# Float32 matmuls against three float32r matmuls of halves in a retention kernel on TensorE

## The chip, the cores and the metric

The kernel runs on one core of a Trainium2 chip. The metric is the device time of one execution in microseconds (us), taken as the median of several runs; lower is better. A profiled execution on the chip is also at hand, with the start and duration of every instruction on every engine: TensorE (PE, and PEld for its weight loads), VectorE (DVE), ScalarE (ACT), GpSimd (POOL) and SyncE (SP), which here only issues transfers.

## The reference, cut to what matters

The program is two layers of a hybrid model and a third block, on 512 positions of width 1024, all in float32. A layer normalises x, multiplies it by a wide weight matrix, and feeds three branches: a depthwise convolution of 31 taps, a retention branch with 4 heads, and windowed attention. The change touches retention alone:

```
q = rotary(q, positions, RET_THETA, RET_QK_DIM)      # 4 heads of 256
k = rotary(k, positions, RET_THETA, RET_QK_DIM)      # then k / 16
scores = einsum('bhnid,bhnjd->bhnij', qc, kc) * decay_inner
inner  = einsum('bhnij,bhnjv->bhniv', scores, vc)    # v: 512 per head
...                                                  # forward and backward, summed
mu  = mean(o, axis=-1); var = mean(square(o - mu))
o   = (o - mu) * rsqrt(var + EPS) * silu(gate)
```

The kernel computes forward and backward, and the parts between chunks, in one product: a full 512 x 512 matrix of scores per head, each multiplied by a decay that depends on the distance of its two positions alone. The mean over the value dimension is taken off v beforehand.

## The kernel before, in words

**Weights.** All weight matrices come as 478 slabs of 128 x 1024. SP brings a slab into one of two `raw` buffers; ACT rounds it to float32r (`high`, L911, into `whi`, four buffers); POOL subtracts (`low`, L292, into `wlo`); and PE multiplies in three float32r matmuls, high by high, high by low and low by high (`gemm`, L359 to L361). Eight such triples, 24 matmuls of 512 columns, make a slab's product, in one of the four PSUM banks `gem`. A bank is free again when its semaphore `evac` has counted the read of it. A `raw` buffer is free when POOL has made the low half from it.

**A head of retention.** Each engine has its own program, and semaphores tie them together. For head hd: PE makes four slabs of q and k, ACT copies them to `QK` (`qk_tick`); DVE rotates them in place (`rope`, L1726 to L1732), with `TT` for scratch; PE makes the values in four slabs over all four banks, ACT copies them with their sums to `VT` (`values`, L1052); DVE takes off the mean (`center_values`, L1759). Then `gates`: PE alternates the four gate slabs with four score tiles (`scores`, L492, two matmuls each of k by q, in the banks `xp` 2 and 3) and four value products (`pv`, L503, four matmuls each, in `xp` 0 and 1). DVE makes the argument of the decay (`decay_arg`, L1716 and L1718), ACT its exponential `DT` (L1062), and DVE multiplies each score tile by it into `ST` (`mask_scores`, L1738). ACT reads the products into `OT` and squares them; DVE adds the squares, PE sums them over partitions (`var`), ACT makes the root, DVE the gated halves (`gated`), and PE multiplies by the output weights (`ret_out`, four slabs of halves in all four banks), which DVE adds to `yr` (`add_out`). The scores and the value products are the matmuls in float32; they take their operands from `U`, one large scratch tile that `QK`, `OT`, `ST`, `SG`, `TT`, `VT` and `DT` are parts of.

**Order.** Heads 0 to 2 of a layer are turns of a loop (`Fori`) that holds the gates of head hd, the q, k and values of head hd + 1, and the output product of head hd; head 3 follows apart. In the same time DVE does the convolution by taps, one instruction each, in PSUM: the first four of eight channel tiles before the first head (`early_conv`, L1655, in pieces between the GLU products), the last four in the heads (`conv`, L1702, 27 taps behind the masking, the last four behind the sum of squares). Everything on an engine runs in the order in which it is written. A turn on DVE is decay_arg, mask_scores, conv, sum_squares, gate_products, conv, rope of q, gated, rope of k, center_values, add_out.

**Idle tiles.** `zhi` and `zlo`, eight tiles of 512 columns each, hold in this stage only the gated halves (tiles 0 to 3) and the sum of squares (tile 7). In layer 1 they are called `hhi` and `hlo`.

Of the kernel before, what the change touches and what calls it, by code (L numbers as in the profile page):

```python
# [19 lines left out]
P = 128  # L20
# [11 lines left out]
HEAD_CUT = 27  # L32
PLAIN = 4
# [41 lines left out]
def build(nc, ins, out, xsave):  # L75
# [5 lines left out]
    with ctx:  # L81
# [24 lines left out]
        U = sb("U", [P, U_SIZE])  # L106
        gem = ctx.enter_context(nc.psum_tensor("gem", [P, 4, T], f32))
# [24 lines left out]
        VT = tiles(U_VT, 4)  # L132
        DT = U[:, U_DT:U_DT + 896]
# [52 lines left out]
        def sem(name):  # L186
# [29 lines left out]
            "v_done", "v_sums", "v_ready", "score_done", "st_ready"))  # L216
        vt_done, vt_ready = sem("vt_done"), sem("vt_ready")
# [123 lines left out]
        def _(pe):  # L341
# [81 lines left out]
            def layer(L):  # L423
# [61 lines left out]
                def scores(hd, j):  # L485
                    n = L * 16 + hd * 4
                    if j == 0:
                        pe.wait_ge(roped, L * 8 + hd * 2 + 2)
                    if j >= 2:
                        pe.wait_ge(st_ready, n + (j - 1))  # L490
                    for r in range(2):
                        mm = pe.matmul(xp[:, 2 + j % 2, :], QK[:, 2 + r, j * P:(j + 1) * P], QK[:, r, :],  # L492
                                       start=(r == 0), stop=(r == 1))
                    mm.then_inc(score_done, 1)

                def pv(hd, v):
                    if v == 0:
                        pe.wait_ge(v_ready, L * 4 + hd + 1)
                        pe.wait_ge(st_ready, L * 16 + hd * 4 + 4)
                    if v >= 2:  # L500
                        pe.wait_ge(o_ready, L * 16 + hd * 4 + (v - 1))
                    for j in range(4):
                        mm = pe.matmul(xp[:, v % 2, :], VT[:, j, v * P:(v + 1) * P], ST[:, j, :],  # L503
                                       start=(j == 0), stop=(j == 3))
# [16 lines left out]
                def var(hd):  # L521
                    pe.wait_ge(ossq, L * 4 + hd + 1)
                    pe.matmul(xp[:, 1, :], ones_r[:, :], zhi[:, 7, :], start=True, stop=False)
                    pe.matmul(xp[:, 1, :], ones_r[:, :], zlo[:, 7, :], start=False, stop=True)\
# [371 lines left out]
        def _(act):  # L896
# [91 lines left out]
            def layer(L):  # L988
                g0, u0 = L * LAYER_GROUPS, L * LAYER_USES

                act.wait_ge(consts, 7)
# [52 lines left out]
                def values(G, hd):  # L1044
                    for k in range(4):
                        high(G, 4 + k + 3)
                    for tb in range(4):
# [6 lines left out]
                    act.drain().then_inc(v_sums, 1)  # L1054

# [4 lines left out]
                def gates(G, hd):  # L1060
# [3 lines left out]
                    for k in range(4):  # L1064
# [6 lines left out]
                        read(k, SG[:, k, :], A.Silu)  # L1071
                    log_exp()
# [11 lines left out]
                values(G, 0)  # L1084
                with act.Fori(0, 3) as hd:
# [9 lines left out]
                    values(G + 1, hd + 1)  # L1095
                    for k in range(4):
# [402 lines left out]
        def _(dve):  # L1499
# [117 lines left out]
            def layer(L):  # L1617
# [70 lines left out]
                early_conv(EARLY_GLU * EARLY_PIECE, EARLY * TAPS)  # L1688
# [31 lines left out]
                def rope(G, u, r):  # L1720

                    x1, x2 = QK[:, 2 * r, :], QK[:, 2 * r + 1, :]
                    cos, sin = tab[:, 0, :], tab[:, 1, :]
                    dve.wait_ge(evac[2 * r], u + 1 + PRIMED)
                    dve.wait_ge(evac[2 * r + 1], u + 1 + PRIMED)
                    tt(TT[:, 0, :], x1, cos, O.mult)  # L1726
                    tt(TT[:, 1, :], x2, sin, O.mult)
                    tt(TT[:, 2, :], x2, cos, O.mult)
                    tt(TT[:, 3, :], x1, sin, O.mult)
                    dve.drain()  # L1730
                    tt(x1, TT[:, 0, :], TT[:, 1, :], O.subtract)
                    tt(x2, TT[:, 2, :], TT[:, 3, :], O.add).then_inc(roped, 1)  # L1732

                def mask_scores(hd):
                    dve.wait_ge(dt_ready, L * 4 + hd + 1)
                    for j in range(4):
                        dve.wait_ge(score_done, L * 16 + hd * 4 + (j + 1))
                        tt(ST[:, j, :], xp[:, 2 + j % 2, :], DT[:, 384 - j * P:896 - j * P], O.mult)\  # L1738
                            .then_inc(st_ready, 1)

                def sum_squares(hd):
# [7 lines left out]
                    dve.tensor_copy(zhi[:, 7, :], TT[:, 2, :])  # L1749
# [705 lines left out]
```

## Time and profile before

| | |
|---|---|
| median of 3 runs | 3052.14 us (3050.22 to 3052.88) |
| span of the profiled execution, first to last instruction | 3048.6 us |
| PE busy | 3016.2 us (99%), 13900 matmul records |
| DVE busy | 1695.3 us (56%) |
| ACT busy | 1132.5 us (37%) |
| POOL busy | 1412.8 us (46%) |
| mean granted clock of TensorE | 0.998 |

The profiled execution's own time is known only by its span; the median of the runs lies 3.5 us above that. Busy is the time in which an engine has at least one instruction under way. Matmuls overlap (a record of a 512-column float32r matmul lasts 0.39 us while the next starts earlier), so paces are read from starts and not from durations.

### The profile page before, as it was taken

What the parts mean: (1) busy time and instruction counts of PE and PEld (TensorE: products, weight loads), DVE (VectorE), ACT (ScalarE), POOL (GpSimd) and SP (SyncE); (2) the same over time, 40 slices, a digit from 0 to 9 for tenths busy, and PEclk for the clock granted to TensorE, in tenths of its full rate; (3) what the DMA queues carried; (4) which work ended last, traced back from release to release, by engine and by line L of the source; (5) the groups of instructions that cost most, each with busy time, mean ns of one, the idle gap of its engine ahead of it and who ended that gap; (6) DMA issues with size and microseconds to landing.
All of it is one profiled execution on the core that took longest, in us unless ns stands there. A gap on an engine that the chain in (4) does not pass through costs nothing.

```text
span 3048.6 us, 41069 instructions
## 1 busy us (share of the span) xinstructions
PE 3016.2 (99%) x13900; PEld 2394.0 (79%) x13900; DVE 1695.3 (56%) x2607; ACT 1132.5 (37%) x1714; POOL 1412.8 (46%) x1040
## 2 busy tenths in 40 slices
PE   8999999999999999999999999999999999999998
PEld 6877877877888887777777788878888888788886
DVE  7974575675434597576577644267772253621214
ACT  4233332365332423233245534236563333422223
POOL 5443543455555453443444555453434444454544
PEclk9999999999999999999999999999999999999999
DMA  4222222212222332222221132221213323233222
GB/s 149 97 69 69 96 69 79 87 43 84 97 97 96 127 104 69 97 72 66 83 90 56 36 131 96 93 100 63 83 62 103 98 83 104 83 103 97 96 97 90
DMA packets 73270, 267.87 MB, mean 88 GB/s; under 512 B 8128, under 2 KB 9024, under 8 KB 72768
## 3 DMA queue, kind: packets, MB, share of 16 engines
q1 hardware_dynamic: 70560, 254.84, 25.3%
q10 hardware_dynamic: 2592, 11.46, 1.0%
q8 instruction: 74, 1.21, 0.2%
q14 instruction: 44, 0.36, 0.0%
HBM read 262.07 MB, written 4.19 MB: 87 GB/s over the span
## 4 chain that ended last, share of the span: by engine, by line
PE 83%; issue 7%; POOL 5%; DVE 3%; DVEq 1%; ACT 0%; POOLq 0%; ACTq 0%
PE gem L359 18%; PE gem L361 18%; PE gem L360 18%; POOL wlo L292 5%; PE xp L503 4%; PE gem L749 2%; PE gem L751 2%; PE gem L750 2%; PE xp L492 2%; PE gem L480 2%; PE gem L479 2%; PE gem L478 2%; PE gem L592 2%; PE gem L615 1%; PE xp L651 1%
## 5 line engine op out<-in xcount | busy, mean ns | idle before, releaser
L292 POOL TENSOR_TENSOR wlo<-raw,whi 128x512 fp32r<-128x512 f32 x956 | 1317.4, 1400 | 1571.9 <-ACT whi L911 1571.3
L911 ACT ACTIVATE whi<-raw 128x1024 fp32r<-128x1024 f32 x478 | 504.6, 1056 | 678.2 <-PE gem L361 462.2
L359 PE MATMUL gem<-zhi,whi 128*128 128x512 f32 x1680 | 664.8, 396 | 0.3 <-DVE zlo L1513 0.3
L361 PE MATMUL gem<-zhi,wlo 128*128 128x512 f32 x1680 | 654.0, 389 | 0.0
L360 PE MATMUL gem<-zlo,whi 128*128 128x512 f32 x1680 | 653.7, 389 | 0.0
L359 PE MATMUL gem<-hhi,whi 128*128 128x512 f32 x1296 | 514.1, 397 | 0.0
L361 PE MATMUL gem<-hhi,wlo 128*128 128x512 f32 x1296 | 504.5, 389 | 0.0
L360 PE MATMUL gem<-hlo,whi 128*128 128x512 f32 x1296 | 504.3, 389 | 0.0
L359 PEld LDWEIGHTS gem<-zhi,whi 128*128 128x128 f32 x1680 | 315.5, 188 | 70.8 <-issue 6.0
L360 PEld LDWEIGHTS gem<-zlo,whi 128*128 128x128 f32 x1680 | 315.5, 188 | 70.0 <-issue 5.5
L361 PEld LDWEIGHTS gem<-zhi,wlo 128*128 128x128 f32 x1680 | 315.4, 188 | 66.1
L359 PEld LDWEIGHTS gem<-hhi,whi 128*128 128x128 f32 x1296 | 243.3, 188 | 55.4 <-issue 5.8
L360 PEld LDWEIGHTS gem<-hlo,whi 128*128 128x128 f32 x1296 | 243.4, 188 | 54.8 <-issue 5.3
L361 PEld LDWEIGHTS gem<-hhi,wlo 128*128 128x128 f32 x1296 | 243.3, 188 | 51.0
L920 ACT ACTIVATE U<-gem 128x512 f32<-128x512 f32 x150 | 89.2, 597 | 459.5 <-PE gem L361 437.0
L1702 DVE SCALAR_TENSOR_TENSOR xp<-cv,sm,xp 128x512 f32<-128x512 f32 x224 | 159.1, 752 | 17.2 <-issue 15.0
L1655 DVE SCALAR_TENSOR_TENSOR xp<-cv,vec,xp 128x512 f32<-128x512 f32 x224 | 159.1, 753 | 9.9 <-issue 0.9
L920 ACT ACTIVATE U<-gem,vec 128x512 f32<-128x512 f32 x96 | 65.6, 685 | 233.9 <-PE gem L361 210.5
L2266 DVE TENSOR_TENSOR U<-gem,U 128x512 f32<-128x512 f32 x22 | 15.2, 692 | 185.5 <-PE gem L361 185.5
L503 PE MATMUL xp<-U 128*128 128x512 f32 x256 | 112.4, 592 | 0.0
L749 PE MATMUL gem<-zhi,whi 128*128 128x512 f32 x256 | 106.5, 416 | 0.5 <-POOL wlo L292 0.5
L301 POOL TENSOR_SCALAR U<-U,sm 128x384 f32<-128x384 f32 x64 | 82.1, 1294 | 42.4 <-DVE sm L1898 42.4
(331 smaller groups left out, 3958.5 us busy)
## 6 DMA issues: line engine op xcount, KB each, us to landing
raw<-in_slabs SPq DMA_DIRECT2D x478, 512.0 KB, 3.5
U<-in_x SPq DMA_DIRECT2D x4, 512.0 KB, 7.5
U<-in_x ACTq DMA_DIRECT2D x1, 2048.0 KB, 8.4
xsave<-U ACTq DMA_DIRECT2D x1, 2048.0 KB, 6.5
U<-xsave ACTq DMA_DIRECT2D x1, 2048.0 KB, 8.3
out_y<-yr SPq DMA_DIRECT2D x8, 256.0 KB, 2.2
tab<-in_tab_ret ACTq DMA_DIRECT2D x2, 512.0 KB, 7.8
tab<-in_tab_att ACTq DMA_DIRECT2D x2, 512.0 KB, 3.6
```

Of the source, the lines that this page charges most:

```text
L292: part = pool.tensor_tensor(wlo[:, k % 4, c], raw[:, k % 2, c], whi[:, k % 4, c].bitcast(f32), O.subtract)
L301: last = pool.tensor_scalar(PB[c][hf], PB[c][hf], REC[c][:, hf:hf + 1], None, O.mult)
L359: pe.matmul(o, wh, hi, start=(n == 0), stop=False)
L360: pe.matmul(o, wh, lo, start=False, stop=False)
L361: mm = pe.matmul(o, wl, hi, start=False, stop=(n == len(terms) - 1))
L478: pe.matmul(o, hhi[:, k, c], wh, start=(k == 0), stop=False)
L503: mm = pe.matmul(xp[:, v % 2, :], VT[:, j, v * P:(v + 1) * P], ST[:, j, :], start=(j == 0), stop=(j == 3))
L749: pe.matmul(gem[:, k, :], wh, hhi[:, r, :], start=(r == 0), stop=False)
L911: act.activation(whi[:, k % 4, :], raw[:, k % 2, :], A.Copy).then_inc(hi_done, 1)
L920: act.activation(dst, gem[:, b, :], func, bias=bias, scale=scale).then_inc(evac[b], 1)
L1655: stt(acc if n < TAPS - 1 else TT[:, 0, :], v, w, acc, O.mult, O.add)
L1702: stt(acc if n < TAPS - 1 else TT[:, 0, :], v, w, acc, O.mult, O.add)
```

## The change

Scores and value products are made in three float32r matmuls of halves each. For this q and k are split after rope (ACT the high half into `zhi` 4 to 7, DVE the low half into `zlo` 4 to 7), the masked scores too (DVE multiplies in place in PSUM, ACT writes the high half and DVE the low half of two tiles at a time, into tiles 0 to 3), and the centred values (high halves over `QK`, low halves over `ST`, by a second name `Ur` of the scratch tile). The sum of squares moves from tile 7 to tile 0. PE waits for two masked tiles at a time. Rope works on both halves of q or of k at once, in two instructions of 1024 columns and two of 512. The last 7 taps of `early_conv` move behind the first rope. In the loop, ACT makes the high half of q before its copies for the values, and that of k in their middle.

```diff
+LATE = 7
+        Ur = nc.alloc_sbuf_tensor_at("Ur", [P, U_SIZE], f32r, offset=nc.sbuf_base - 4 * U_SIZE)
+        VHI, VLO = (Ur[:, a:a + 4 * T].rearrange("p (a b) -> p a b", a=4) for a in (U_A, U_C))
...
                 def scores(hd, j):
                     if j == 0:
-                        pe.wait_ge(roped, L * 8 + hd * 2 + 2)
+                        pe.wait_ge(qk_ready, L * 8 + hd * 2 + 2)
                     if j >= 2:
-                        pe.wait_ge(st_ready, n + (j - 1))
+                        pe.wait_ge(st_ready, L * 8 + hd * 2 + 1)
+                    o, c = xp[:, 2 + j % 2, :], slice(j * P, (j + 1) * P)
                     for r in range(2):
-                        mm = pe.matmul(xp[:, 2 + j % 2, :], QK[:, 2 + r, j * P:(j + 1) * P], QK[:, r, :],
-                                       start=(r == 0), stop=(r == 1))
+                        pe.matmul(o, zhi[:, 6 + r, c], zhi[:, 4 + r, :], start=(r == 0), stop=False)
+                        pe.matmul(o, zhi[:, 6 + r, c], zlo[:, 4 + r, :], start=False, stop=False)
+                        mm = pe.matmul(o, zlo[:, 6 + r, c], zhi[:, 4 + r, :], start=False, stop=(r == 1))
...
                 def pv(hd, v):
-                        pe.wait_ge(st_ready, L * 16 + hd * 4 + 4)
+                        pe.wait_ge(st_ready, L * 8 + hd * 2 + 2)
...
                     for j in range(4):
-                        mm = pe.matmul(xp[:, v % 2, :], VT[:, j, v * P:(v + 1) * P], ST[:, j, :],
-                                       start=(j == 0), stop=(j == 3))
+                        pe.matmul(o, VHI[:, j, c], zhi[:, j, :], start=(j == 0), stop=False)
+                        pe.matmul(o, VHI[:, j, c], zlo[:, j, :], start=False, stop=False)
+                        mm = pe.matmul(o, VLO[:, j, c], zhi[:, j, :], start=False, stop=(j == 3))
...
+                def qk_highs(hd, r):
+                    act.wait_ge(roped, L * 8 + hd * 2 + (r + 1))
+                    act.activation(zhi[:, 4 + 2 * r:6 + 2 * r, :], QK[:, 2 * r:2 * r + 2, :], A.Copy).then_inc(qk_high, 1)
-                def values(G, hd):
+                def values(G, hd, mid=False):
                     for k in range(4):
                         high(G, 4 + k + 3)
+                        if mid and k == 1:
+                            qk_highs(hd, 1)
...
+                def value_highs(hd):
+                    act.wait_ge(v_mean, L * 4 + hd + 1)
+                    for tb in range(4):
+                        act.activation(VHI[:, tb, :], VT[:, tb, :], A.Identity, bias=VM[:, tb:tb + 1]).then_inc(v_high, 1)
...
                         read(k, SG[:, k, :], A.Silu)
+                        if k < 2:
+                            act.wait_ge(st_mul, L * 8 + hd * 2 + (k + 1))
+                            act.activation(zhi[:, 2 * k:2 * k + 2, :], xp[:, 2:4, :], A.Copy).then_inc(st_high, 1)
...
                 values(G, 0)
+                qk_highs(0, 0)
+                qk_highs(0, 1)
+                value_highs(0)
...
                     qk_tick(G + 1, 3)
-                    values(G + 1, hd + 1)
-                    for k in range(4):
+                    qk_highs(hd + 1, 0)
+                    values(G + 1, hd + 1, True)
+                    high(G + 3, 3)
+                    value_highs(hd + 1)
+                    for k in range(1, 4):
                         high(G + 3, k + 3)
...
-                early_conv(EARLY_GLU * EARLY_PIECE, EARLY * TAPS)
+                early_conv(EARLY_GLU * EARLY_PIECE, EARLY * TAPS - LATE)
+                def late_conv():
+                    early_conv(EARLY * TAPS - LATE, EARLY * TAPS)
...
+                def rope_low(hd, r):
+                    dve.wait_ge(qk_high, L * 8 + hd * 2 + (r + 1))
+                    c = slice(4 + 2 * r, 6 + 2 * r)
+                    tt(zlo[:, c, :], QK[:, 2 * r:2 * r + 2, :], zhi[:, c, :].bitcast(f32), O.subtract).then_inc(qk_ready, 1)
 
                 def mask_scores(hd):
                     dve.wait_ge(dt_ready, L * 4 + hd + 1)
-                    for j in range(4):
-                        dve.wait_ge(score_done, L * 16 + hd * 4 + (j + 1))
-                        tt(ST[:, j, :], xp[:, 2 + j % 2, :], DT[:, 384 - j * P:896 - j * P], O.mult)\
-                            .then_inc(st_ready, 1)
+                    for a in range(2):
+                        for j in range(2 * a, 2 * a + 2):
+                            dve.wait_ge(score_done, L * 16 + hd * 4 + (j + 1))
+                            o = xp[:, 2 + j % 2, :]
+                            last = tt(o, o, DT[:, 384 - j * P:896 - j * P], O.mult)
+                        last.then_inc(st_mul, 1)
+                        dve.drain()
+                        dve.wait_ge(st_high, L * 8 + hd * 2 + (a + 1))
+                        c = slice(2 * a, 2 * a + 2)
+                        tt(zlo[:, c, :], xp[:, 2:4, :], zhi[:, c, :].bitcast(f32), O.subtract).then_inc(st_ready, 1)
...
                 def center_values(hd):
                     dve.wait_ge(v_sums, L * 4 + hd + 1)
-                    ts(VM, VS, -1.0 / T, None, O.mult)
+                    ts(VM, VS, -1.0 / T, None, O.mult).then_inc(v_mean, 1)
                     dve.drain()
                     for tb in range(4):
-                        last = ts(VT[:, tb, :], VT[:, tb, :], VM[:, tb:tb + 1], None, O.add)
+                        dve.wait_ge(v_high, L * 16 + hd * 4 + (tb + 1))
+                        last = stt(VLO[:, tb, :], VT[:, tb, :], VM[:, tb:tb + 1], VHI[:, tb, :].bitcast(f32),
+                                   O.add, O.subtract)
...
                 rope(G, u, 0)
-                dve.drain()
                 rope(G, u, 1)
+                rope_low(0, 0)
+                rope_low(0, 1)
+                late_conv()
                 dve.drain()
                 center_values(0)
...
                     rope(G + 1, u + 1, 0)
                     gated(hd)
+                    rope_low(hd + 1, 0)
                     rope(G + 1, u + 1, 1)
+                    rope_low(hd + 1, 1)
```

How this moves instructions on DVE before the first head of layer 0, from the last taps of the early convolution to centring. Before (L1655 and L1660 are taps and their closing sum, L1726 to L1732 rope, L1756 and L1759 centring):

```order
L1655 SCALAR_TENSOR_TENSOR xp<-cv,vec,xp 128x512 x28
L1655 SCALAR_TENSOR_TENSOR U<-cv,vec,xp 128x512
L1660 SCALAR_TENSOR_TENSOR cv<-xp,vec,U 128x512
L1726 TENSOR_TENSOR U<-U,tab 128x512
L1727 TENSOR_TENSOR U<-U,tab 128x512
L1728 TENSOR_TENSOR U<-U,tab 128x512
L1729 TENSOR_TENSOR U<-U,tab 128x512
L1731 TENSOR_TENSOR U<-U 128x512
L1732 TENSOR_TENSOR U<-U 128x512
```

And with the change, from the same tap on (L1686 and L1691 taps and sum, L1760 to L1764 rope, L1771 the low halves of q and k, L1801 and L1805 centring); the rope of k repeats the four rows of that of q:

```order
L1686 SCALAR_TENSOR_TENSOR xp<-cv,vec,xp 128x512 x22
L1760 TENSOR_TENSOR U<-U,tab 128x1024
L1761 TENSOR_TENSOR U<-U,tab 128x1024
L1763 TENSOR_TENSOR U<-U 128x512
L1764 TENSOR_TENSOR U<-U 128x512
...
L1771 TENSOR_TENSOR zlo<-U,zhi 128x1024 x2
L1686 SCALAR_TENSOR_TENSOR xp<-cv,vec,xp 128x512 x6
L1686 SCALAR_TENSOR_TENSOR U<-cv,vec,xp 128x512
L1691 SCALAR_TENSOR_TENSOR cv<-xp,vec,U 128x512
L1801 TENSOR_SCALAR sm<-sm 128x4
L1805 SCALAR_TENSOR_TENSOR Ur<-U,sm,Ur 128x512 x4
```

Six taps, the last tap and the closing sum now stand between rope and centring; `decay_arg` still follows centring.

On ACT, in the loop, from the copy that follows the root of the variance (L928 reads q and k) to the reads of the values (L1068). With the change:

```order
L928 ACTIVATE U<-gem 128x512
L1056 ACTIVATE zhi<-U 128x1024
L919 ACTIVATE whi<-raw 128x1024
...
L919 ACTIVATE whi<-raw 128x1024
L1056 ACTIVATE zhi<-U 128x1024
...
L919 ACTIVATE whi<-raw 128x1024
...
L919 ACTIVATE whi<-raw 128x1024
...
L1068 ACTIVATE U,sm<-gem 128x512
```

Before, the same stretch had the four weight copies (L911) in a row and the four reads (L1052) behind them:

```order
L920 ACTIVATE U<-gem 128x512
L911 ACTIVATE whi<-raw 128x1024
...
L911 ACTIVATE whi<-raw 128x1024
...
L911 ACTIVATE whi<-raw 128x1024
...
L911 ACTIVATE whi<-raw 128x1024
...
L1052 ACTIVATE U,sm<-gem 128x512
```

The two copies of 1024 columns (L1056) are new; the second stands between the second and the third weight copy and waits for the rope of k.

## Rows read from the trace of the kernel before

**Rows 1.** The page: busy time, and the chain that ended last.

```profile
PE 3016.2 (99%) x13900; PEld 2394.0 (79%) x13900; DVE 1695.3 (56%) x2607; ACT 1132.5 (37%) x1714; POOL 1412.8 (46%) x1040
...
PE 83%; issue 7%; POOL 5%; DVE 3%; DVEq 1%; ACT 0%; POOLq 0%; ACTq 0%
```

**Rows 2.** PE's groups by form: records, busy us, mean ns, idle before.

```profile
L503 PE MATMUL xp<-U 128*128 128x512 f32 x256 | 112.4, 592 | 0.0
...
L492 PE MATMUL xp<-U 128*128 128x512 f32 x128 | 57.6, 593 | 0.7 <-DVE U L1732 0.7
```

**Rows 3.** PE's timeline, first head of layer 0: start us, us, instruction, idle before.

```profile
149.89 0.39 PE L361 MATMUL gem<-hhi,wlo 128*128 128x512 f32 x1
...
153.29 0.39 PE L361 MATMUL gem<-hhi,wlo 128*128 128x512 f32 x1
154.38 3.70 PE L492 MATMUL xp<-U 128*128 128x512 f32 x8 [0.71 <-DVE U L1732]
...
163.41 3.59 PE L492 MATMUL xp<-U 128*128 128x512 f32 x8
...
167.07 0.40 PE L360 MATMUL gem<-hlo,whi 128*128 128x512 f32 x1
...
184.62 7.03 PE L503 MATMUL xp<-U 128*128 128x512 f32 x16
```

**Rows 4.** DVE's timeline, from the early taps to the second head's centring.

```profile
122.69 20.94 DVE L1655 SCALAR_TENSOR_TENSOR xp<-cv,vec,xp 128x512 f32<-128x512 f32 x28
...
145.52 1.60 DVE L1726 TENSOR_TENSOR U<-U,tab 128x512 f32<-128x512 f32 x1 [0.24 <-issue]
...
154.67 1.67 DVE L1759 TENSOR_SCALAR U<-U,sm 128x512 f32<-128x512 f32 x4
...
157.41 1.15 DVE L1718 SCALAR_TENSOR_TENSOR U<-dist,sm,U 128x896 f32<-128x896 int16 x1 [0.19 <-issue]
159.67 1.29 DVE L1738 TENSOR_TENSOR U<-xp,U 128x512 f32<-128x512 f32 x2 [1.11 <-ACT U L1062]
...
194.59 0.69 DVE L1744 TENSOR_TENSOR U<-U 128x512 f32<-128x512 f32 x1 [4.91 <-ACT U L1079]
...
208.73 0.69 DVE L1726 TENSOR_TENSOR U<-U,tab 128x512 f32<-128x512 f32 x1 [0.26 <-PE xp L524]
...
227.92 1.78 DVE L1728 TENSOR_TENSOR U<-U,tab 128x512 f32<-128x512 f32 x1
...
230.98 0.69 DVE L1732 TENSOR_TENSOR U<-U 128x512 f32<-128x512 f32 x1
236.45 0.17 DVE L1756 TENSOR_SCALAR sm<-sm 128x4 f32<-128x4 f32 x1 [4.78 <-ACTq L1054]
```

**Rows 5.** ACT's timeline, first head of layer 0.

```profile
148.77 0.19 ACT L1052 ACTIVATION_READ_ACCUMULATOR U<-gem 128x1 f32 x1
158.60 0.95 ACT L1062 ACTIVATE U<-U 128x896 f32<-128x896 f32 x1 [9.63 <-DVE U L1718]
159.57 1.28 ACT L1063 ACT_TABLE_LOAD   x1
160.86 1.06 ACT L911 ACTIVATE whi<-raw 128x1024 fp32r<-128x1024 f32 x1
161.83 0.58 ACT L920 ACTIVATE U<-gem 128x512 f32<-128x512 f32 x1
```

**Rows 6.** PE's timeline behind an idle gap.

```profile
2059.85 0.79 PE L387 MATMUL gem<-zhi,whi 128*128 128x512 f32 x1 [4.91 <-DVE zlo L1581]
...
2063.32 0.39 PE L389 MATMUL gem<-zhi,wlo 128*128 128x512 f32 x1
```

**Rows 7.** A window there: busy of PE, PEld, DVE, ACT, POOL; clock; DMA.

```profile
2060.00:2062.00 2.00, 2.00 (x5) 1.61 (x6) 1.91 (x4) 2.00 (x4) 0.50 (x1) 0.50 0.00 0
```

**Rows 8.** POOL's timeline in the same head: one slab's low half.

```profile
225.96 3.19 POOL L292 TENSOR_TENSOR wlo<-raw,whi 128x512 fp32r<-128x512 f32 x2 [2.25 <-ACT whi L911]
```

**Rows 9.** The page's DMA issues: count, size, median us to landing.

```profile
raw<-in_slabs SPq DMA_DIRECT2D x478, 512.0 KB, 3.5
```

More of the change, by code:

```diff
@@ L216, in build @@
             "v_done", "v_sums", "v_ready", "score_done", "st_ready"))
+        qk_high, qk_ready, v_mean, v_high, st_mul, st_high = (sem(n) for n in (
+            "qk_high", "qk_ready", "v_mean", "v_high", "st_mul", "st_high"))
         vt_done, vt_ready = sem("vt_done"), sem("vt_ready")
@@ L498, in pv @@
                         pe.wait_ge(v_ready, L * 4 + hd + 1)
[L499 removed]
+                        pe.wait_ge(st_ready, L * 8 + hd * 2 + 2)
                     if v >= 2:
                         pe.wait_ge(o_ready, L * 16 + hd * 4 + (v - 1))
+                    o, c = xp[:, v % 2, :], slice(v * P, (v + 1) * P)
                     for j in range(4):
[L503 to L504 removed]
+                        pe.matmul(o, VHI[:, j, c], zhi[:, j, :], start=(j == 0), stop=False)
+                        pe.matmul(o, VHI[:, j, c], zlo[:, j, :], start=False, stop=False)
+                        mm = pe.matmul(o, VLO[:, j, c], zhi[:, j, :], start=False, stop=(j == 3))
                     mm.then_inc(pv_done, 1)
@@ L522, in var @@
                     pe.wait_ge(ossq, L * 4 + hd + 1)
-                    pe.matmul(xp[:, 1, :], ones_r[:, :], zhi[:, 7, :], start=True, stop=False)
-                    pe.matmul(xp[:, 1, :], ones_r[:, :], zlo[:, 7, :], start=False, stop=True)\
+                    pe.matmul(xp[:, 1, :], ones_r[:, :], zhi[:, 0, :], start=True, stop=False)
+                    pe.matmul(xp[:, 1, :], ones_r[:, :], zlo[:, 0, :], start=False, stop=True)\
                         .then_inc(ovar, 1)
@@ L989, in layer @@
                 g0, u0 = L * LAYER_GROUPS, L * LAYER_USES
+                zhi = Z[L][0]
                 act.wait_ge(consts, 7)
@@ L1720, in rope @@
                 def rope(G, u, r):
-                    x1, x2 = QK[:, 2 * r, :], QK[:, 2 * r + 1, :]
-                    cos, sin = tab[:, 0, :], tab[:, 1, :]
+                    x = QK[:, 2 * r:2 * r + 2, :]
+                    cos, sin = (tab[:, n:n + 1, :].to_broadcast([P, 2, T]) for n in range(2))
                     dve.wait_ge(evac[2 * r], u + 1 + PRIMED)
                     dve.wait_ge(evac[2 * r + 1], u + 1 + PRIMED)
-                    tt(TT[:, 0, :], x1, cos, O.mult)
-                    tt(TT[:, 1, :], x2, sin, O.mult)
@@ L1728, in rope @@
-                    tt(TT[:, 2, :], x2, cos, O.mult)
-                    tt(TT[:, 3, :], x1, sin, O.mult)
+                    tt(TT[:, 0:2, :], x, cos, O.mult)
+                    tt(TT[:, 2:4, :], x, sin, O.mult)
                     dve.drain()
-                    tt(x1, TT[:, 0, :], TT[:, 1, :], O.subtract)
-                    tt(x2, TT[:, 2, :], TT[:, 3, :], O.add).then_inc(roped, 1)
+                    tt(QK[:, 2 * r, :], TT[:, 0, :], TT[:, 3, :], O.subtract)
+                    tt(QK[:, 2 * r + 1, :], TT[:, 1, :], TT[:, 2, :], O.add).then_inc(roped, 1)
```

6 lines of the change are left out of this document (3 added, 3 removed).

## The prediction

> **What bounds the kernel now.** I read the page's shares first and the chain of waits second: PE is busy for 99% of the span and carries 83% of the chain [rows 1]. A microsecond taken from PE's stream is therefore a microsecond of time, as long as PE is not made to wait instead; and every other engine has idle time, so the question about each of them is only whether it is late for PE. Third, PE's groups by form: the two float32 products that the change replaces, L503 and L492, stand there with 256 and 128 records [rows 2]. The diff has 8 score and 16 value matmuls for each of 4 heads in 2 layers, so 64 and 128 of them: a float32 matmul leaves two records. Fourth, the timelines of one head, for the paces and for how late each engine is.
>
> **The saving on PE.** The products of halves around the scores start at 149.89, ..., 153.29, which is 15 steps of 0.2267 us [rows 3]. The scores' four float32 matmuls start at 163.41, and the next product's second matmul starts at 167.07, its first so at 166.84: 3.43 us for four, 0.8575 each. Three matmuls of halves would take 3 x 0.2267 = 0.680. So 0.1775 saved for each of 192: **34.1 us**. A group of two score tiles goes from 3.43 to 2.72, of two value tiles from 6.86 to 5.44, and a head's four gate slabs with their groups from 42.3 to 38.1 us. The wait of the first scores for rope (0.71 idle, 154.38 against a slab that ended at 153.52: 0.86 in all [rows 3]) goes too, if the halves of q and k are there by 153.5: **0.9 us**, in layer 0 alone.
>
> The Trainium skill (TensorE: Matmul & The Clock Gate, Back-to-back issue gap) gives 215.7 ns between matmuls of 512 columns where these rows have 226.7; by the page's figure the saving would be 40.4 us by an estimate from it. The row is of the same form as the new matmuls, and I take the row.
>
> **What it costs at the first head of each layer.** Times are layer 0's. Today the conv taps that fill VectorE before rope end at 145.3 and rope starts at 145.52 [rows 4]. LATE = 7 moves seven taps and the closing sum, eight instructions of 20.94/28 = 0.75 with drains, 6.1 us, behind rope and its low halves. Rope now starts near 139.3; it is the same elements in fewer instructions, about 4 us for each of q and k and up to 2 more from GpSimd, so it ends between 148 and 150.5. ScalarE is free at 149.0 (148.77 + 0.19 [rows 5]). Its two copies of 1024 columns cost about 1.0 each (L911 has the same form, 160.86 to 161.83 [rows 5]). The two subtractions of 1024 columns are priced at two of 0.69 less overlap, 1.25 (between 1.2 and, with GpSimd in the way of each, 2.3). q and k are ready near 152.8, just ahead of PE's 153.5.
>
> Now the late taps: 152.8 + 6.1 = 159.0, where centring's four additions started at 154.67 before. Centring no longer runs alone: VectorE makes the mean (0.2), ScalarE the first high half (0.6), VectorE four low halves (0.7 each): 162.8. The decay argument ends 2.2 later (center_values ended at 156.34 and L1718 at 158.56): 165.0. ScalarE: exp 1.0, table load 1.3, whi copy 1.0, gate read 0.5, then the new high half of two score tiles 1.05, with VectorE's low half 1.25 behind it: 171.1. Before, from the end of exp to the first masked tile was 0.8 us [rows 4, 5]. PE, which now waits at the third score tile for the low half of both first tiles, is there at 153.5 + 2.72 + 5.44 = 161.7. So it stands for about **9.3 us**, where today it doesn't stand at all: the first masked tile was ready near 160.3 and PE came for it at 163.41, a slack of 3.1 that the change eats three times over. Layer 1 repeats the pattern: 18.6 in both. Bounds of one such stall, from the unknown prices (1024-column operations on PSUM, GpSimd's interference, the read of four tiles): 8 to 11.5.
>
> What follows a stall. At 2054.95 PE stopped, and went on at 2059.85 after 4.91 idle; the granted clock from 2060 to 2062 was 0.50, the 1.2 GHz level; the ninth start after it came at 2063.32, so eight steps took 3.47 where 1.81 is the full pace [rows 6, 7]. That is 1.7 us lost, and a stall of 9.3 is longer than this one. So **3.4 us** for two. The Trainium skill (TensorE: Matmul & The Clock Gate, HAM oscillation) says the same of gaps between bursts of matmuls, and speaks against this change: a saving in matmuls bought with one long gap pays for the gap and for the slow start behind it. Without the fall of the clock the sum would be 3.4 lower.
>
> **What it costs in the loop of heads.** Call E the end of a head's value products (before: 184.62 + 6.86 = 191.48 [rows 3]). Gates: the two scores groups have their low half 2 us before PE needs them (mask, ScalarE 1.05, VectorE 1.25 against a slab of 5.44), because in the loop the decay argument is not late. VectorE's taps start later relative to E by the masks' new step (about 1.1 after the last mask, and PE's groups are shorter): the sum of squares moves from E + 3.1 to about E + 3.6 and uses up its wait of 4.9 us on the squares; rope of the next q moves from E + 17.25 to E + 17.5 [rows 4]. Rope of k ended at 231.66 = E + 40.2, and 4.8 us idle followed [rows 4]. In between, ScalarE must now make the high half of k in the middle of four whi copies, so it stands still until rope of k is done, and the last two whi copies and the four reads of values queue behind that. The added low half of q delays rope by 1.3; but rope of k took 6.0 with two multiplications at 1.78 in place of 0.69 while GpSimd made a low half from 225.96 [rows 4, 8], and that low half now waits for the very copy that waits for rope, so it is out of the way: 2.2 back. I put rope's end between E + 39.7 and E + 40.8. Then ScalarE 1.0 (high half), 2.0 (two whi), 0.6 (first tile of values): bank 0 is free between E + 43.3 and E + 44.4, and PE wants it at E + 44.0 (eight slabs of 24 matmuls, 5.44 each, and the variance pair's 0.45). A wait of 0 to 0.4; I take 0.2, for six heads **1.1 us** (bounds 0 to 6: one further collision with GpSimd is 1.1). Behind the values the whi copy of the last output slab waits for its transfer (3.5 us to landing [rows 9], its buffer freed only near E + 44.7), the high halves of v queue behind it, and the first two added outputs leave banks 0 and 1 near E + 54.2 with PE there at E + 54.9. That costs nothing, by 0.7 us. The fourth head has no such successor, and conv_done leaves 10 us to spare.
>
> **The sum.** -34.1 - 0.9 + 18.6 + 3.4 + 1.1 = -11.9. The profiled span is 3048.6, so 3036.7; the median of the three runs is 3052.14, 3.5 above the span, so **3040.2 us**.
>
> **The rivals.**
> - *The first heads' wait is hidden.* If the decay argument came before the late taps, or these were covered, the 22 us of stall and clock would go: -35.0 + 1.1, so 3018. For it: LATE takes 6.1 off rope's path. Against: in the order of VectorE the argument still stands behind the taps and the centring, and 6.2 us of ScalarE and VectorE work lie between it and the third score tile. A half-way case (the stall is 5 or 6, since ScalarE's pieces overlap more than I let them) gives 3030.
> - *ScalarE's place in the loop becomes the wait; slower than before.* ScalarE stands for rope of k. If rope ends at E + 43 rather than E + 40.3 (GpSimd in the way of three more operations of 1024 columns, which hold it longer than 512), PE waits 2.7 at bank 0 in six heads, and from there each further microsecond is six. The point from which it decides is 11.9 / 6 = 2.0 us above my value, rope at E + 42.3; at E + 43.0, 3044 + 12 = 3056. For it: the margins are 0.7 and the Pool's collisions cost 1.1 each. Against: 4.8 us of idle VectorE in today's rows, and the collision that removes itself.
> - *The clock stays up over the stalls.* 3036.8. Against it: the row of 4.91.
> - *Halves on these tiles run slower than 0.2267, so that the change doesn't do what it says.* It would need 0.286 each to save nothing. The variance pair's rows and every slab's have 0.2267; I see nothing for it.
>
> **How the numbers follow.** The forecast as it stands (stalls of 8 to 11.5, loop within 0 to 1 each) 0.60, 3034 to 3047. Hidden or half hidden wait 0.18, 3017 to 3034. Loop wait 0.15, of which two thirds end within or under the old time plus 6 and one third above. Clock stays up 0.04; no saving 0.03. About 0.2% (6 us) is what a measurement of this kernel tells from no change. Faster by more: 0.60 + 0.18 + 0.04 less 0.02 of the forecast's own edge, and a little of the loop case, 0.81; within: 0.12; slower: 0.07. The range, 3024 to 3051, leaves out a tenth on each side.
>
> **What would show it.** In the profile after: the new scores' and values' matmuls start 0.227 apart; PE idle of about 9 us before the third score tile in the first head of each layer, released by VectorE's low half of scores (and nothing like it in the other heads); starts about 0.43 apart for some 3.5 us behind each of the two, at half the granted clock; no wait for rope before the first scores; a distance from head to head in the loop that is 4.3 us shorter than before; ScalarE idle some 11 us before the high half of k, with PE waiting under 0.5 for the bank of the first values. It is wrong if PE's idle time at the first heads is under 7 or over 12, or if the loop's heads show waits of over 1 us.

## The result and the profile after

The changed kernel took 3069.24 us (median of 4 runs, 3068.69 to 3070.56) against 3051.88 before (that median has one more run than the table above): the ratio is 1.0059, with an interval from 1.0047 to 1.0071. It is 17 us slower where 12 us faster was forecast, and it lies outside the range. The profiled span grew from 3048.6 to 3067.3 us.

The page of the changed kernel, its shares and its chain, which answer to [rows 1]:

```profile
PE 2999.9 (98%) x14092; PEld 2438.7 (80%) x14092; DVE 1760.8 (57%) x2607; ACT 1180.6 (38%) x1778; POOL 1424.9 (46%) x1040
...
PE 59%; issue 24%; POOL 15%; DVE 1%; ACT 1%; POOLq 0%; DMA 0%; DVEq 0%; ACTq 0%; SPq 0%
```

PE has less work by 16 us and still ends 19 us later, so it waits more, and part of what is left of its work is slower. The waits of PE alone, from the same trace (line, what it waited for, total us, times, longest):

```profile
PE gem L364 <- DVE yr L1834: 13.7, 6, 2.4
PE gem L443 <- DVE zlo L1638: 11.9, 2, 11.0
PE xp L497 <- DVE zlo L1784: 9.2, 1, 9.2
PE xp L497 <- DVE hlo L1784: 8.9, 1, 8.9
...
PE gem L364 <- ACT U L1068: 4.7, 5, 1.0
```

L443 is the start of the program and was there before (12.7 us). The other four rows are new and make 36.5 us. Two are the wait at the third score tile of the first head of each layer, as forecast. The others stand in the loop: before the third slab of the output product, where PE waits until VectorE has added the first slab's outputs (six heads), and before the first slab, where it waits until ScalarE has read the values.

PE's timeline in the first head of layer 0. It answers to [rows 3]:

```profile
153.27 0.39 PE L497 MATMUL xp<-zhi 128*128 128x512 f32 x1
...
155.77 0.39 PE L499 MATMUL xp<-zhi,zlo 128*128 128x512 f32 x1
...
170.81 0.80 PE L497 MATMUL xp<-zhi 128*128 128x512 f32 x1 [9.21 <-DVE zlo L1784]
...
175.67 0.63 PE L499 MATMUL xp<-zhi,zlo 128*128 128x512 f32 x1
...
182.00 0.39 PE L510 MATMUL xp<-zhi,Ur 128*128 128x512 f32 x1
```

The first pair of tiles runs its 12 matmuls at (155.77 - 153.27) / 11 = 0.227 us, the pace that the forecast took, and there is no wait for rope ahead of it. The second pair comes 9.21 late and runs at 0.43: its last start is 175.67, so it ends at 176.10 and takes 5.29 in place of 2.72, and the slab behind it 5.90 in place of 5.44. The windows say what the clock did (the figure after POOL's count):

```profile
161.50:170.80 9.30, 0.10 (x1) 0.00 (x0) 5.39 (x7) 6.08 (x8) 2.63 (x3) 0.78 0.00 1
170.80:176.10 5.30, 5.29 (x13) 4.13 (x14) 0.70 (x1) 0.13 (x1) 2.33 (x2) 0.50 0.58 192
176.10:182.00 5.90, 5.90 (x25) 4.83 (x24) 4.20 (x6) 1.97 (x2) 2.54 (x2) 0.92 0.02 8
```

All of the second pair ran at half of the full clock, the 1.2 GHz level. The fall cost 2.57 + 0.46 = 3.0 us here. In layer 1, behind a wait of 8.9, the clock rose again before the pair was done: the pair took 4.65 us and the slab behind it its usual 5.44, so the fall cost 1.9.

```profile
1197.10:1201.80 4.70, 4.66 (x13) 3.70 (x14) 0.70 (x1) 0.17 (x1) 2.37 (x2) 0.58 0.57 172
```

Now the loop. PE's timeline at the output product of the second and third head of layer 0:

```profile
351.03 0.50 PE L364 MATMUL gem<-zhi,whi 128*128 128x512 f32 x1 [0.89 <-ACT U L1068]
...
364.61 0.69 PE L364 MATMUL gem<-zhi,whi 128*128 128x512 f32 x1 [2.36 <-DVE yr L1834]
...
368.35 0.39 PE L364 MATMUL gem<-zhi,whi 128*128 128x512 f32 x1
```

The nine steps from 364.61 to 368.35 take 3.74 us in place of 2.04: a wait of 2.36 us costs 1.70 more behind it. The wait of 0.89 has no such tail. From the first score matmul of one head to that of the next the distance was 108.2 us before and should have become 103.9; it is 120.1 after the first head (153.27 to 273.34) and 109.3 after the next (273.34 to 382.67). The distances that follow are 109.4 in layer 0, and 120.4, 109.5 and 109.2 in layer 1.

```profile
273.34 0.39 PE L497 MATMUL xp<-zhi 128*128 128x512 f32 x1
...
382.67 0.39 PE L497 MATMUL xp<-zhi 128*128 128x512 f32 x1
```

VectorE's and ScalarE's timelines from rope of k to the added outputs in the first head show why; they answer to the last rows of [rows 4] and to [rows 5]. VectorE:

```profile
237.36 0.68 DVE L1764 TENSOR_TENSOR U<-U 128x512 f32<-128x512 f32 x1
239.17 1.23 DVE L1771 TENSOR_TENSOR zlo<-U,zhi 128x1024 fp32r<-128x1024 f32 x1 [1.13 <-ACT zhi L1056]
243.40 0.66 DVE L1801 TENSOR_SCALAR sm<-sm 128x4 f32<-128x4 f32 x1 [3.01 <-ACTq L1070]
248.27 6.36 DVE L1805 SCALAR_TENSOR_TENSOR Ur<-U,sm,Ur 128x512 fp32r<-128x512 f32 x4 [4.21 <-ACT Ur L1076]
254.56 2.47 DVE L1834 TENSOR_TENSOR yr<-gem,yr 128x512 f32<-128x512 f32 x4
```

ScalarE, and GpSimd below it:

```profile
238.07 1.06 ACT L1056 ACTIVATE zhi<-U 128x1024 fp32r<-128x1024 f32 x1 [10.81 <-DVE U L1764]
239.04 2.00 ACT L919 ACTIVATE whi<-raw 128x1024 fp32r<-128x1024 f32 x2
...
246.57 1.06 ACT L919 ACTIVATE whi<-raw 128x1024 fp32r<-128x1024 f32 x1 [3.23 <-DMA raw<-in_slabs]
247.53 2.55 ACT L1076 ACTIVATE Ur<-U,sm 128x512 fp32r<-128x512 f32 x4
249.99 1.04 ACT L919 ACTIVATE whi<-raw 128x1024 fp32r<-128x1024 f32 x1
```

```profile
247.70 3.00 POOL L297 TENSOR_TENSOR wlo<-raw,whi 128x512 fp32r<-128x512 f32 x2 [2.42 <-ACT whi L919]
251.11 2.98 POOL L297 TENSOR_TENSOR wlo<-raw,whi 128x512 fp32r<-128x512 f32 x2 [0.40 <-ACT whi L919]
```

With E = 198.32 for this head, rope of k ended at E + 39.7, the early edge of what was forecast. ScalarE stood 10.8 us for it, so the transfer of a later slab was late, and ScalarE's weight copy waited for that transfer until E + 48.2, as forecast too. The high halves of v queued behind it. Then VectorE's four low halves of v took 6.36 us, where the forecast's E + 54.2 leaves them about 2.8: GpSimd was at its own low halves from 247.70 to 254.09 with a pause of 0.4 us, and each of the four met it. The Trainium skill (SBUF — State Buffer, Who interferes with whom) has it that a VectorE instruction with two inputs in SBUF contends with a GpSimd instruction that reads SBUF; the rows agree, at 1.6 against 0.7 us each. The first added output came at 255.2, E + 56.9, and PE, there at E + 54.9, waited.

### The profile page after: what moved, and what is told of

Its sections match the earlier page's. It is cut to its first block, busy times and chain, and to the rows that moved or that the text cites. A ratio compares the mean times of both kernels' runs of the same rounds, so it can differ in the third digit from the quotient of the medians.

```text
span 3067.3 us, 41636 instructions
## 1 busy us (share of the span) xinstructions
PE 2999.9 (98%) x14092; PEld 2438.7 (80%) x14092; DVE 1760.8 (57%) x2607; ACT 1180.6 (38%) x1778; POOL 1424.9 (46%) x1040
## 4 chain that ended last, share of the span: by engine, by line
PE 59%; issue 24%; POOL 15%; DVE 1%; ACT 1%; POOLq 0%; DMA 0%; DVEq 0%; ACTq 0%; SPq 0%
POOL wlo L297 15%; PE gem L364 13%; PE gem L366 13%; PE gem L365 13%; PE gem L757 2%; PE gem L759 2%; PE gem L758 2%; PE gem L600 2%; PE gem L623 1%; PE xp L659 1%; PE gem L602 1%; PE gem L601 1%; PE xp L643 1%; PE xp L766 0%; PE gem L443 0%
## 5 line engine op out<-in xcount | busy, mean ns | idle before, releaser
L366 PE MATMUL gem<-zhi,wlo 128*128 128x512 f32 x1680 | 655.6, 390 | 0.0
L366 PEld LDWEIGHTS gem<-hhi,wlo 128*128 128x128 f32 x1296 | 244.3, 189 | 51.5
L928 ACT ACTIVATE U<-gem 128x512 f32<-128x512 f32 x150 | 89.3, 597 | 412.1 <-PE gem L366 389.6
L1686 DVE SCALAR_TENSOR_TENSOR xp<-cv,vec,xp 128x512 f32<-128x512 f32 x224 | 159.1, 752 | 9.9 <-issue 0.9
L928 ACT ACTIVATE U<-gem,vec 128x512 f32<-128x512 f32 x96 | 65.6, 685 | 236.7 <-PE gem L366 213.2
L759 PE MATMUL gem<-zhi,wlo 128*128 128x512 f32 x256 | 100.2, 391 | 0.0
```

Source lines behind the costliest of these rows:

```text
L366: mm = pe.matmul(o, wl, hi, start=False, stop=(n == len(terms) - 1))
L759: mm = pe.matmul(gem[:, k, :], wl, hhi[:, r, :], start=False, stop=(r == NT - 1))
L928: act.activation(dst, gem[:, b, :], func, bias=bias, scale=scale).then_inc(evac[b], 1)
L1686: stt(acc if n < TAPS - 1 else TT[:, 0, :], v, w, acc, O.mult, O.add)
```

## The experiments

The kernels named e1 to e3 and e5 to e7 are variants of the changed kernel, e4 of the kernel before. Beside e1 to e4 the kernel before took 3051.76 us, and beside e5 to e7, which ran on another chip, 3050.90.

**e1_swap: the high halves of v ahead of the weight copy.**

```diff
-                    high(G + 3, 3)
                     value_highs(hd + 1)
-                    for k in range(1, 4):
+                    for k in range(4):
                         high(G + 3, k + 3)
```

> The changed kernel with one pair of ScalarE's steps exchanged in the loop: the high halves of v come ahead of the weight copy of the last output slab, which waits for its transfer. Theory A (the added outputs are late because the high halves of v queue behind that weight copy, and behind it VectorE's low halves meet GpSimd's): VectorE's low halves of v start near E + 45.5 instead of E + 50, the wait of PE for VectorE's added outputs (2 to 2.4 us in six heads) is gone, and with it the fall of the clock behind it (1.6 to 1.7 us each): 6 x 3.9 = 23 us less, 3046 us. PE's waits for ScalarE's read of the values (0.9 in two heads a layer) and of 9.2 at the first head stay. Rival B (the low halves of v are slow by themselves, 1.6 us each wherever they stand, and it is their length that makes the outputs late): they now end near E + 52.5, still ahead of 54.9, so the waits go too, but the low halves stay at 6.4 us; under A they are near 3 to 4.5. Rival C (the outputs are late for another reason, such as PE's own earlier stall): the wait stays and the time is within 5 us of 3069.

Measured: 3044.51 us, ratio to before 0.9978 (0.9968 to 0.9988). That is 24.7 us off the changed kernel by two lines, and turns it from slower to slightly faster. The wait for VectorE's added outputs is gone from the waits; PE's, of this kernel:

```profile
PE xp L497 <- DVE zlo L1783: 9.2, 1, 9.2
PE xp L497 <- DVE hlo L1783: 8.9, 1, 8.9
PE gem L364 <- ACT U L1068: 5.6, 6, 1.0
```

VectorE's low halves of v take less than half as long:

```profile
246.26 2.97 DVE L1804 SCALAR_TENSOR_TENSOR Ur<-U,sm,Ur 128x512 fp32r<-128x512 f32 x4 [0.79 <-ACT Ur L1076]
```

Theory A holds, and rival B falls: four low halves took 2.97 us and not 6.36, so their length was a matter of where they stood. One number of the expectation missed: they start at E + 48.3 (E is 198.0 here) and not near 45.5, 1.7 us earlier than in the changed kernel; the high half of k, ahead of them, now came 1.8 later. In the other loop heads they start 3.2 to 3.5 us earlier. So this run moved the start and the length of the low halves together, and does not tell by the waits alone which of the two made the outputs late; e2_reads does. 13.7 us of waits and six falls of the clock at about 1.7 make 23.9 of the 24.7. The waits of 9.2 and 8.9 at the first heads are those of the changed kernel, yet the clock behind them cost only 1.5 and 1.6 us in place of 3.0 and 1.9.

**e2_reads: also the high half of k behind the reads of the values.**

```diff
-                    values(G + 1, hd + 1, True)
+                    values(G + 1, hd + 1)
+                    qk_highs(hd + 1, 1)
```

> As e1_swap, and also the high half of k moved from the middle of the weight copies to behind the four reads of the values. Theory A (ScalarE standing for rope of k holds up the weight copies, the transfers and the reads): ScalarE no longer stands, PE's wait for the first values' read (0.9 us in two heads a layer, 4 in all) goes too; 4 to 5 us less than e1_swap, 3041 us. Rope of k meets GpSimd again and ends 2 us later, which costs nothing. Rival: the low half of k now comes so late that centring and the added outputs are late: a wait of 1 us or more for VectorE's added outputs, 3050 or more. In both the waits of 9.2 us at the two first heads stay.

Measured: 3038.34 us, 0.9957 (0.9940 to 0.9973), 6.2 less than e1_swap where 4 to 5 was expected: each wait of 0.9 to 1.0 had made its head 1.2 to 1.3 longer (105.1 against 103.84 us from head to head). No wait of PE is left in the loop. Rope of k met GpSimd and took until 243.86, as expected, at no cost:

```profile
240.18 2.31 DVE L1761 TENSOR_TENSOR U<-U,tab 128x1024 f32<-128x1024 f32 x1
...
247.34 2.74 DVE L1805 SCALAR_TENSOR_TENSOR Ur<-U,sm,Ur 128x512 fp32r<-128x512 f32 x4 [0.79 <-ACT Ur L1076]
250.00 1.28 DVE L1834 TENSOR_TENSOR yr<-gem,yr 128x512 f32<-128x512 f32 x2
```

Here the low halves of v start at E + 49.35, almost where they did in the changed kernel (E + 49.95), but ahead of GpSimd's work and not beside it, and take 2.74 us; the first added output comes at E + 52.7 in place of 56.9. All 32 of them in this trace lie clear of GpSimd's instructions and take 0.74 to 0.76 us; in the changed kernel 24 of the 32 lie beside them and take 1.27 to 1.79, and the 8 that do not take 0.74 to 0.75. So it is the meeting with GpSimd that made the outputs late, and not the start. In the later loop heads of the changed kernel, where the low halves start at E + 51.5 to 51.7 and PE comes at about E + 56.3, the same holds by an estimate: with 2.74 for them and 0.6 for the first output it would be there at E + 55.

This is the kernel that the forecast described, with the first heads' waits and none in the loop: it was put at 3039 (3040.2 less the 1.1 for the loop), and is at 3038.3. The clock at the two first heads cost 1.6 and 1.7 here, as forecast.

**e3_order: the late taps behind the decay argument, the loop as in the changed kernel.**

```diff
                 rope_low(0, 1)
-                late_conv()
                 dve.drain()
                 center_values(0)
...
+                decay_arg(0)
+                late_conv()
                 with dve.Fori(0, 3) as hd:
-                    decay_arg(hd)
                     mask_scores(hd)
...
+                    decay_arg(hd + 1)
```

> The changed kernel with only VectorE's order altered at the first head of each layer: rope, low halves, centring, decay argument, then the 7 late taps, where the late taps stood ahead of centring. Theory (the chain from the taps over the decay argument, exp, table load, weight copy and gate read to the halves of the scores sets PE's wait of 9.2 us): now ScalarE's part (about 4 us) lies beside the taps; the third score tile's wait is 6.5 to 7 us in place of 9.2, the clock falls as before, and the time is 2 x 2.5 = 5 us less, 3064. Rival (the wait is set by something else, such as the number of VectorE instructions behind PE): unchanged, 3069. The loop's waits stay as they are.

Measured: 3065.77 us, 1.0048 (1.0031 to 1.0064), so 3.5 less than the changed kernel. The two waits are 6.5 and 6.2 us in place of 9.2 and 8.9, and the loop's stay:

```profile
PE gem L364 <- DVE yr L1834: 14.0, 6, 2.4
...
PE xp L497 <- DVE zlo L1784: 6.5, 1, 6.5
PE xp L497 <- DVE hlo L1784: 6.2, 1, 6.2
```

The chain over the decay argument sets the wait, as the theory has it. The time fell by 2 us less than the waits did. The traces say where: the six distances from head to head are together 6.9 us shorter (115.7, 109.3, 109.4 and 117.9, 109.3, 109.4), of which 1.4 is a fall of the clock that did not come behind the first loop wait of 2.16 us; but 3.2 is lost outside the heads, in stretches that the edit does not touch, most of it where the clock was low for longer, behind waits at the start of the program (1.2) and behind the gap of 4.9 that all these kernels have (1.4). The spans differ by 3.7.

**e4_pad10: the price of a short wait, in the kernel before.**

```diff
                     center_values(hd + 1)
+                    for n in range(10):
+                        dve.drain()
+                        stt(xp[:, 2 + n % 2, :], cv[:, 7, 0:T], EPS, xp[:, 2 + n % 2, :], O.mult, O.add)
                     add_out(G + 3, u + 3)
```

> The kernel before with ten idle VectorE instructions of 0.83 us ahead of the added outputs of each loop head; it computes the same. It prices a short wait of PE by itself: VectorE frees bank 0 near E + 56.9 where PE comes at E + 54.9, a wait of about 2.0 us in six heads. If a short wait costs its length alone: 12 us more than before. If the clock falls behind it as in the changed kernel (half pace for 3.5 us, 1.6 to 1.7 lost): 6 x 3.7 = 22 us more. The granted clock is 0.5 for some 3.5 us behind each wait in the second case.

Measured, in one run: 3072.35 us, 20.6 above the kernel before; the spans differ by 22.0. PE waited 1.83 us in each of six heads. Its timeline at the first of them:

```profile
249.13 0.50 PE L359 MATMUL gem<-zhi,whi 128*128 128x512 f32 x1 [1.83 <-DVE yr L1787]
249.47 0.40 PE L360 MATMUL gem<-zlo,whi 128*128 128x512 f32 x1
249.71 0.58 PE L361 MATMUL gem<-zhi,wlo 128*128 128x512 f32 x1
...
253.35 0.40 PE L361 MATMUL gem<-zhi,wlo 128*128 128x512 f32 x1
```

```profile
251.00:253.00 2.00, 2.00 (x6) 1.60 (x5) 0.00 (x0) 0.00 (x0) 0.00 (x0) 0.50 0.42 100
```

The clock fell about half a microsecond after PE had gone on, to the 1.2 GHz level. 11 steps from 249.13 to 253.35 took 4.22 us where 2.49 is the full pace, so 1.73 on top of the wait. But it did not fall behind every one of the six, though all six waits are 1.83 or 1.84 us long. Behind the third the starts keep to 0.227 apart and the clock is full:

```profile
472.93 0.50 PE L359 MATMUL gem<-zhi,whi 128*128 128x512 f32 x1 [1.83 <-DVE yr L1787]
...
474.00:476.00 2.00, 2.00 (x10) 1.66 (x9) 0.67 (x2) 0.00 (x0) 0.81 (x1) 1.00 0.06 6
```

From head to head the distance grew by 3.7 to 3.8 us in four cases and by 2.1 in two (the third and the fifth), where the clock stayed up. So a wait of 1.83 costs 2.1 by itself, a fall of the clock 1.6 more, and the six come to 19.2 of the 22.0; the other 2.8 lie in stretches that the edit does not touch. The second case of the expectation holds for four of six waits, in a kernel that has nothing of the change; that its number came out is in part luck.

**e5_all: e2_reads with the first head's small steps put in order.** The first turn of the loop is written out on VectorE and ScalarE, and in every head the decay argument and its exponential come at the end of the head before: in the first turn VectorE masks the first pair of score tiles, centres the values, makes the pair's low half, and only then runs the late taps and masks the second pair. The core of it (the middle part is in mask_scores):

```diff
                 rope_low(0, 1)
-                late_conv()
-                dve.drain()
-                center_values(0)
+                decay_arg(0)
+                value_means(0)
...
+                        if a and between is not None:
+                            late_conv()
...
+                        if a == 0 and between is not None:
+                            between()
...
                 qk_highs(0, 1)
+                decay(0)
                 value_highs(0)
+                score_highs(0, 0)
```

> e2_reads with the first head of each layer written out apart from the loop. VectorE makes the decay argument and the means ahead of everything else, masks the first two score tiles, then centres the values, then makes the low half of the scores, and only then the 7 late taps, ahead of the second pair; ScalarE makes the exponential ahead of the high halves of v and the first high half of the scores ahead of its table load. Theory (the order of small steps on two engines makes the 9.2 us wait at the third score tile, and the fall of the clock behind it costs another 3.0): the first low half of scores is ready near 160.6 in layer 0, PE comes at 161.4, no wait; the second pair may be late by 0 to 1 us. So 2 x 12.2 us less than e2_reads, less 0 to 2: 3014 to 3016 us, which is 36 below the kernel before, the 34 of the matmuls and the first wait. Rival (part of the saving is not there: matmuls of halves on these tiles lose time in another place): a time above 3019 with no wait of PE in the first heads.

Measured: 3018.34 us, 0.9895 (0.9878 to 0.9911): the fastest of all, 32.6 us under the kernel before and 50.9 under the changed one. VectorE in the first head of layer 0, and PE's wait there:

```profile
155.68 1.30 DVE L1794 TENSOR_TENSOR xp<-xp,U 128x512 f32<-128x512 f32 x2 [1.00 <-ACT U L1084]
157.07 2.74 DVE L1826 SCALAR_TENSOR_TENSOR Ur<-U,sm,Ur 128x512 fp32r<-128x512 f32 x4
159.91 1.22 DVE L1801 TENSOR_TENSOR zlo<-xp,zhi 128x1024 fp32r<-128x1024 f32 x1
161.22 4.39 DVE L1699 SCALAR_TENSOR_TENSOR xp<-cv,vec,xp 128x512 f32<-128x512 f32 x6
```

```profile
170.93 0.47 PE L510 MATMUL xp<-zhi,Ur 128*128 128x512 f32 x1 [1.18 <-DVE zlo L1801]
171.70 0.39 PE L510 MATMUL xp<-zhi,Ur 128*128 128x512 f32 x1
```

The low half was ready at 161.1, with PE there at 161.4. The second pair was 1.2 and 1.1 us late in the two layers, and the clock stayed up over these (three steps from 170.93 to 171.70 took 0.77 against 0.68). With them the sum comes to 3050.9 - 35.0 + 2.5 = 3018.4. The saving of the matmuls is there to within a microsecond: from head to head the distance in the loop is 103.84 us where it was 108.17. The rival falls.

**e6_both: e2_reads with e3_order's order.**

> e2_reads and e3_order together. If waits at different places add up, as the theory has it: e2_reads less the 3.5 us that e3_order took off the changed kernel, 3035 us, with a wait of 6.4 at the first heads and none in the loop. Rival (the waits share a cause): over 3037 or under 3033.

Measured: 3033.97 us, 0.9943 (0.9926 to 0.9959), 4.4 less than e2_reads. The waits at the first heads are 6.5 and 6.2, none is in the loop. The two repairs add up: by the traces the two first heads are 3.9 us shorter than in e2_reads. The waits are 5.4 less there, and the clock behind them took back 1.5 of it.

**e7_late0: e2_reads with LATE = 0.**

> e2_reads with LATE = 0, so that all early taps stand ahead of rope again. Theory (what PE waits for is the whole of VectorE's work up to the scores' low halves, and LATE only says where the wait stands): PE waits about 4 us before the first score tile and about 2 us before the third, in place of 9.2 before the third; the clock falls behind both. Sum about the same or 1 to 3 us a layer shorter, since the first products at half pace run while VectorE works: 3033 to 3038 us. Rival (moving the taps is worth its 6 us a layer): 3044 or more.

Measured: 3030.92 us, 0.9933 (0.9913 to 0.9953), the median of four runs, one of which took 6099.68 us and is no evidence on the kernel. Of the other three the median is 3030.54. That is 7.4 less than e2_reads, 2.1 below the expected range:

```profile
PE xp L497 <- DVE hlo L1784: 3.6, 1, 3.6
PE xp L497 <- DVE zlo L1771: 2.9, 1, 2.9
PE xp L497 <- DVE zlo L1784: 2.1, 1, 2.1
PE xp L497 <- DVE hlo L1771: 1.7, 1, 1.7
```

The rival falls. By the traces the first heads are 2.3 and 3.3 us shorter, near the 1 to 3 a layer of the expectation, and 1.5 of the 7.1 between the two spans lies outside the heads. The clock fell behind three of the four waits and not behind the one of 1.7. The waits sum to 10.3 us in place of 18.1, since VectorE's work goes on while PE runs its first pair; the late taps, as the change places them, cost more than they bring.

## Why the prediction was wrong, point by point

**The saving: right.** 34.1 us by the pace of 0.2267; the changed kernel's rows have 0.227, and e5_all shows 32.6 of 35.0 in the time, with 2.3 us of waits left. From head to head it is 4.33 us, for eight heads 34.6.

**The first wait for rope: right.** It is gone.

**The first heads' wait: right.** 18.6 forecast; 9.2 and 8.9 measured, released by the instruction that was named. e3_order shows its chain and e5_all removes it.

**The clock behind it: right mechanism, in the changed kernel too small.** 1.7 each was read from a row behind a gap of 4.91. The changed kernel lost 3.0 in layer 0 and 1.9 in layer 1, 5.0 in place of 3.4; e1_swap lost 1.5 and 1.6 and e2_reads 1.6 and 1.7, behind waits of the same length. So the length of the wait does not set it. How long the clock stays low behind a wait differs from one case to the next, and what decides it stays open here.

**The loop: wrong, and this is the step that failed.** The prediction said that the first two added outputs "leave banks 0 and 1 near E + 54.2 with PE there at E + 54.9" and that this "costs nothing, by 0.7 us"; waits of over 1 us in the loop's heads were its own sign of being wrong. The chain up to the high halves of v was right to within 0.2 us. The four low halves of v behind them were priced at their duration without GpSimd. They took 6.36 us, and the first output came at E + 56.9. e1_swap moved these ahead of the weight copy and had 2.97; e2_reads had 2.74 from almost the same start. Why they collided could have been read: the weight copy that delays them is itself what starts GpSimd, and the next weight copy follows the high halves, so GpSimd's next two low halves fall exactly beside VectorE's four.

**Short waits priced at their length: the second half of the same error.** The forecast multiplied a loop wait by six heads and added nothing for the clock, though it had done so for the long one. e4_pad10 shows 1.73 us behind a wait of 1.83, in four cases of six. In the loop the clock fell behind all six, and that made 13.7 us of waits for outputs into about 24.

**ScalarE's read of the values: mis-sized.** 1.1 us forecast for six heads, 4.7 measured in five waits of 0.9 to 1.0. By e1_swap each makes its head about 1.25 longer, so 6.2 for five, at the edge of the bound of 0 to 6. e2_reads removed it.

**The sum over again.** Without waits the distance from head to head is 103.84 us (e2_reads, e5_all). The six distances of the changed kernel are 16.2, 5.5, 5.5 and 16.5, 5.6, 5.4 above it. 12.4 of the 16.2 and 11.0 of the 16.5 are the first head's wait and the clock behind it, 23.4 in place of 22.0; the loop has the other 31.4, in place of 1.1. With the saving of 34.6 + 0.9 = 35.5 in place of 35.0 the sum is -11.9 + 1.4 + 30.3 - 0.5 = +19.3, against 18.7 measured in the spans; the last 0.6 lies outside the heads, where the edits of this case change nothing and two traces differ by up to about 3 us. The rival "slower than before" named a bank of the output product that is late behind ScalarE standing for rope of k, and the right multiplier of six; but it meant the read of the values, ahead of the first slab, and a rope later than forecast, and not the added outputs. A time above the old one was given 7 chances in 100.

## What to carry to other kernels

Price an instruction that is moved behind a wait together with what the same wait sets free on the engine that slows it, here GpSimd, and not by its best duration. When PE is 99% busy, a wait of about 2 us on it can cost some 1.7 us of half clock on top of its length (it did behind six of six waits in the changed kernel and four of six in e4_pad10), so a margin of 0.7 us that is passed six times is a risk worth more than the saving. Matmuls taken off PE pay only if each small step of the other engines that PE now waits for is put in order too: the same three matmuls of halves gave +17 us and -33 us.

## What the runs showed of the hardware that was not expected

In the heads, the granted clock of TensorE fell to its 1.2 GHz level behind waits of PE as short as 1.83 us, in e4_pad10 only 0.6 to 1.4 us after PE had gone on at full pace. The length of the wait does not decide it alone: behind the six waits of 1.83 and 1.84 us in e4_pad10 it fell four times and stayed up twice; it stayed up behind one of 2.16 in e3_order and one of 1.73 in e7_late0, and fell behind all six of 1.93 to 2.44 in the changed kernel. Behind waits of 0.9 to 1.2 it never fell. A fall cost PE 1.6 to 1.7 us behind the short waits, and 1.5 to 3.0 behind those of 9 us.

VectorE's low half of v (L1805, 512 columns, which adds the mean and subtracts the high half, both tensors in SBUF) took 0.74 us alone and up to 1.79 while GpSimd made its halves: in the changed kernel the median of all 32 was 1.75 us, in e2_reads 0.75. GpSimd's own pair grew from 2.5 to 3.0 us.
